# Attention of the first layer in pairs of heads, woven between its projections, with probabilities scaled by a diagonal on TensorE

## The chip, the cores and the metric

The kernel runs on one core of one Trainium2 chip. The metric is the time of one execution on the device in microseconds. An execution that was recorded by the hardware profiler shows where the time goes. The engines are TensorE (PE in the rows; its weight loads are PEld), VectorE (DVE), ScalarE (ACT), GpSimd (POOL) and SyncE (SP), whose queue issues nearly all loads.

## The reference

A trunk of two layers on 256 positions of width 1024, in fp32. Each layer is a mixer and a feed-forward block (SwiGLU, inner width 2816), both with norms in front and behind. The second layer's mixer (dilated attention) is not touched except in names. The first is a sparse attention with 16 query heads of 64, 4 key heads, and three branches for every head, each with a sigmoid gate:

```
proj = a @ w_in                                   # q 1024 | six k/v of 256 | gates 48
kc, vc = compress(k_cmp, wk1, wk2), compress(v_cmp, wv1, wv2)   # 15 blocks of 32 positions, stride 16
        # compress: silu(blocks(2048) @ w1(2048x256)) @ w2(256x64)
p_cmp = softmax(mask(q @ kc * scale)) * valid ;  o_cmp = p_cmp @ vc
o_sel = softmax(mask(q_rot @ k_sel * scale)) @ v_sel     # with 256 positions all blocks are selected
o_win = softmax(mask(q_rot @ k_win * scale)) @ v_win     # causal, window 512
o = g_cmp * o_cmp + g_sel * o_sel + g_win * o_win ;  m = o @ w_o
```

## The kernel before

Every engine has its own program, written out by hand; what stands earlier in an engine's program runs earlier, and semaphores order the engines against each other. There is no planner.

**Weights.** They come in pieces of 128x2048 fp32 into a ring of seven slots (`w_raw`). ScalarE writes the rounded high part (`split`, L606), VectorE the rest (`w_lo`, L1073). TensorE multiplies a block in three products, high by high, high by low, low by high (`three`, through `mm`, L1545). A slot is loaded again when `piece_used` says that its products are done. The pieces are in the order of `N_CMPKV ... N_NSAO, N_FFN0`.

**First layer.** The rows of x are transposed (L1554), with the gains `g_t` that come out of one transpose of `rows` (L1610). Then come ten projections of 128 positions by 512 columns (`nsa_gemm`), each 24 products: 0 to 5 for the keys and values, 6 to 9 for the queries. Between them stand the gate product, the turns of keys and queries, and `compress` for the keys and for the values (48 products of 256 columns each, both operands split into high and low).

**Attention.** It follows the last query projection. A unit is one head and one tile m of 128 queries; there are 32. For each unit TensorE makes the scores of both branches in one product (`scores_nsa`, L1738): the keys stand in `k_z` with zeros in the half of the 128 rows that belongs to the other head, so that the contraction is over 128 rows. VectorE adds the mask and takes the minimum of the negated scores (L1284), ScalarE exponentiates and sums (L804), VectorE takes the reciprocal (L1294) and multiplies the probabilities by it and by the gate (L1300). TensorE transposes them in blocks of 128 (`turn_probs`, L1761) into one of two banks, ScalarE copies the bank to `p_t` (L816), and TensorE multiplies by the values (`pv`, L1769), one head in columns 0 to 63 or 64 to 127 of the array, block after block. After each second head it adds the product with the compressed values (L1788). TensorE is three units behind its scores with the transposes and five with the values. GpSimd builds masks.

**Behind it.** `out_proj` (four blocks, 96 products) starts when all heads are done, then the norm and residual (`gain_post`, `add_post`), and the feed-forward block starts with the transposed rows `xt_hi`, `xt_lo` (L615, L1105).

The functions that the change touches, with the line numbers of the rows:

## Time and profile before

| | us |
|---|---|
| median of 3 runs | 864.36 (863.7 to 865.74) |
| the profiled execution | 866.18 |
| its span | 864.4 |
| TensorE busy in the span | 845.2 (98%) |
| VectorE / ScalarE / GpSimd busy | 535.4 / 476.1 / 37.5 |
| first layer's mixer, from the first product of a projection to the first feed-forward product | 11.17 to 191.80 |
| of it the attention | 94.4 to 166.9 |

The profiled execution's time is the one on the device; the span runs from its first recorded instruction to its last. A share of busy time over the whole span says little about a stage, so the rows below are by stretch and by piece. In a chain of waits every line is a piece of the path that ended last. A product of two fp32 operands shows as two records (x2 for one product), one of the rounded fp32r type as one, and a plain transpose as one. The duration of a record reaches past the start of the next; the lengths in the chain do not.

### The profile page before, as it was taken

To read this page: it belongs to the slowest core of one execution; us is meant where nothing else is said; L and a number is where in the kernel's file an instruction comes from. 1 tells how busy PE (TensorE), PEld (TensorE's weight loads), DVE (VectorE), ACT (ScalarE), POOL (GpSimd) and SP (SyncE) were. 2 spreads that over 40 slices of the span, in tenths; PEclk is the share of its full clock that TensorE was granted. 3 is DMA by queue.
4 is the path that set the end of the run, shared out by engine and by line. 5 is a ranking of instruction groups with operands and counts; after the bars stand their busy time and mean duration, and the time that the engine had idled before them with its cause. 6 is when DMAs were issued, how large, how long until landed. Compare 5 with 4: busy or idle time off the path is not lost.

```text
span 864.4 us, 11546 instructions
## 1 busy us (share of the span) xinstructions
PE 845.2 (98%) x4345; PEld 682.8 (79%) x4345; DVE 535.4 (62%) x1136; ACT 476.1 (55%) x862; POOL 37.5 (4%) x120
## 2 busy tenths in 40 slices
PE   6999999999999999999999999999999999999996
PEld 5898766778888888878887888888777888888885
DVE  5987786686655555578455555655566965455544
ACT  7786666664544444465555655665556754444431
POOL 3000018200000000000000000000000000000000
PEclk9999999999999999999999999999999999999999
DMA  9775300044565466468545353535331756645601
GB/s 323 243 258 193 98 1 2 1 156 159 183 228 175 148 219 217 146 197 272 190 155 185 98 183 110 167 126 174 119 98 50 238 187 222 205 147 191 223 24 49
DMA packets 108967, 137.48 MB, mean 159 GB/s; under 512 B 6336, under 2 KB 92400, under 8 KB 108784
## 3 DMA queue, kind: packets, MB, share of 16 engines
q1 hardware_dynamic: 107824, 132.53, 46.1%
q0 software_dynamic: 992, 4.19, 1.3%
q8 instruction: 34, 0.56, 0.3%
q14 instruction: 21, 0.17, 0.1%
q10 hardware_dynamic: 96, 0.02, 0.0%
HBM read 134.64 MB, written 2.10 MB: 158 GB/s over the span
## 4 chain that ended last, share of the span: by engine, by line
PE 92%; DVE 4%; ACT 2%; DMA 1%; issue 0%; ACTq 0%; SPq 0%
PE ps L1545 79%; PE ps L1554 5%; PE ps L1738 3%; PE ps L1769 3%; PE ps L1761 1%; DVE w_lo L1073 1%; DVE xt_lo L1105 1%; PE ps L1788 1%; DMA w_raw<-in_ffn_w_gu 1%; DMA rows<-in_nsa_cmp_pos 1%; ACT w_hi L606 0%; PE ps L1716 0%; ACT xt_hi L615 0%; DVE h L1347 0%; ACT probs L804 0%
## 5 line engine op out<-in xcount | busy, mean ns | idle before, releaser
L1073 DVE TENSOR_TENSOR w_lo<-w_raw,w_hi 128x1024 fp32r<-128x1024 f32 x248 | 296.5, 1222 | 116.1 <-ACT w_hi L606 114.1
L1545 PE MATMUL ps<-w_hi,xt_hi 128*128 128x512 f32 x760 | 309.0, 407 | 3.1 <-DVE xt_lo L1105 2.0
L1545 PE MATMUL ps<-w_hi,xt_lo 128*128 128x512 f32 x760 | 299.0, 393 | 0.0
L1545 PE MATMUL ps<-w_lo,xt_hi 128*128 128x512 f32 x760 | 298.3, 393 | 0.0
L606 ACT ACTIVATE w_hi<-w_raw 128x1024 fp32r<-128x1024 f32 x248 | 253.5, 1058 | 6.1 <-DMA w_raw<-in_ffn_w_gu 6.0
L1545 PEld LDWEIGHTS ps<-w_hi,xt_hi 128*128 128x128 f32 x760 | 144.3, 190 | 32.5 <-DVE xt_lo L1105 2.4
L1545 PEld LDWEIGHTS ps<-w_hi,xt_lo 128*128 128x128 f32 x760 | 144.2, 190 | 31.7
L1545 PEld LDWEIGHTS ps<-w_lo,xt_hi 128*128 128x128 f32 x760 | 144.6, 190 | 26.9
L871 ACT ACTIVATE st_hi<-ps 128x256 fp32r<-128x256 f32 x40 | 15.4, 384 | 116.8 <-PE ps L1554 116.8
L1377 DVE TENSOR_TENSOR st_lo<-ps,st_hi 128x256 fp32r<-128x256 f32 x40 | 17.0, 425 | 75.0 <-ACT st_hi L871 74.8
L1545 PE MATMUL ps<-w_hi,st_hi 128*128 128x512 f32 x160 | 62.6, 391 | 0.0
L1545 PE MATMUL ps<-w_hi,st_lo 128*128 128x512 f32 x160 | 62.3, 389 | 0.0
L1545 PE MATMUL ps<-w_lo,st_hi 128*128 128x512 f32 x160 | 62.3, 389 | 0.0
L804 ACT ACTIVATE probs<-probs,mn 128x128 f32<-128x128 f32 (+2 forms) x96 | 51.4, 537 | 15.5 <-DVE mn L1284 15.5
L866 ACT ACTIVATE silu<-ps,rs 128x256 f32<-128x256 f32 x44 | 20.9, 475 | 66.8 <-PE ps L1545 66.5
L959 ACT ACTIVATE qk_t<-ps 128x256 f32<-128x256 f32 x48 | 15.8, 382 | 53.5 <-PE ps L1554 53.5
L1371 DVE SCALAR_TENSOR_TENSOR hs<-ps,rs,silu 128x256 f32<-128x256 f32 x44 | 21.3, 483 | 34.1 <-ACT silu L866 34.1
L1545 PEld LDWEIGHTS ps<-w_hi,st_lo 128*128 128x128 f32 x160 | 30.0, 188 | 6.3
L1545 PEld LDWEIGHTS ps<-w_lo,st_hi 128*128 128x128 f32 x160 | 30.1, 188 | 6.1
L1545 PEld LDWEIGHTS ps<-w_hi,st_hi 128*128 128x128 f32 x160 | 30.0, 188 | 6.1
L1284 DVE CUSTOM_DVE_ANT_0 probs<-ps,mask_dil 128x512 f32<-128x512 f32 x32 | 20.8, 689 | 22.3 <-PE ps L1545 22.2
L1284 DVE CUSTOM_DVE_ANT_0 probs<-ps,mask_nsa 128x128 f32<-128x128 f32 (+1 forms) x64 | 20.2, 354 | 16.1 <-PE ps L1738 15.3
(206 smaller groups left out, 853.4 us busy)
## 6 DMA issues: line engine op xcount, KB each, us to landing
w_raw<-in_ffn_w_gu SPq DMA_DIRECT2D x88, 512.0 KB, 5.0
w_raw<-in_dil_w_in SPq DMA_DIRECT2D x72, 512.0 KB, 4.7
w_raw<-in_ffn_w_down SPq DMA_DIRECT2D x44, 512.0 KB, 4.7
w_raw<-in_nsa_w_in SPq DMA_DIRECT2D x20, 512.0 KB, 6.1
w_raw<-in_nsa_w_o SPq DMA_DIRECT2D x8, 512.0 KB, 4.7
w_raw<-in_dil_w_o SPq DMA_DIRECT2D x8, 512.0 KB, 4.5
w_raw<-in_nsa_cmp_wk SPq DMA_DIRECT2D x4, 512.0 KB, 9.7
w_raw<-in_nsa_cmp_wv SPq DMA_DIRECT2D x4, 512.0 KB, 6.7
```

The lines of the kernel that those rows point to most:

```text
L606: act.activation(w_hi[:, n.slot, c:c + 1024], w_raw[:, n.slot, c:c + 1024], ACT.Copy)\
L804: ins = act.activation(p, p, ACT.Exp, bias=mn[:, w % 4, br:br + 1], scale=-1.0, accum_out=l_u[:, w % 4, br:br + 1])
L866: act.activation(silu[:, m, :], bank(gu_bank(j, m), 0, 256), ACT.Silu, scale=rs[:, m:m + 1])\
L959: ins = act.activation(view(qk_t, (qk_slot(x.g, x.pat) * 4 + 2 * t) * S + x.m * 64, [[S, 2], [P, 2], [1, 64]]), view(ps, (2 + x.qk_no % 2) ...
L1073: dve.tensor_tensor(w_lo[:, n.slot, c:c + 1024], w_raw[:, n.slot, c:c + 1024], w_hi[:, n.slot, c:c + 1024].bitcast(F32), ALU.subtract)\
L1284: ins = dve.tensor_tensor_reduce(out=probs[:, w % 4, br * n:(br + 1) * n], in0=bank(score_bank(w) if b is None else b, br * n, n), in1=mas ...
L1371: dve.scalar_tensor_tensor(hs[:, m, :], bank(gu_bank(j, m), 256, 256), rs[:, m:m + 1], silu[:, m, :], ALU.mult, ALU.mult).then_inc(hs_read ...
L1377: dve.tensor_tensor(view(st_of(j)[1], m * P, [[S, 2], [1, P]]), bank(6 + m, 0, 256).rearrange("p (a t) -> p a t", a=2), hi.bitcast(F32), A ...
L1545: ins = pe.matmul(o, s, m, start=start, stop=stop)
L1554: ins = pe.transpose(ps[0:n, b, P * k:P * k + P], src, ident[:, :])
L1738: pe.matmul(bank(score_bank(u), 0, 2 * n), q_t[:, hd // 2, m * P:(m + 1) * P], k_z[:, hd % 2, :, hd // G, 0:n], start=True, stop=True).the ...
L1769: ins = pe.matmul(o, v, p_t[:, w % 4, P * k:P * k + P], start=k == 0, stop=i == 1 and k == len(vs) - 1, skip_group_check=i == 0)
```

## The change

Four things change, all in the first layer's mixer.

1. *Pairs.* The 32 units become 16 pairs of heads (`pair_nsa`: half r of the heads, tile m, pair j). Both heads of a pair stand in one tile of 128 rows of `q_t` and `k_both`, and their scores are products over 64 rows each, the one in rows 0 to 63, the other in 64 to 127, into two banks. The values are multiplied with the two heads alternating between the column halves. The products with the compressed values come four at a time, once for four pairs.
2. *Unscaled probabilities.* VectorE no longer multiplies the probabilities. It makes gate over sum, four numbers a pair and row; GpSimd multiplies the identity by them (`diag`, 128x512), and TensorE multiplies each block of probabilities by its diagonal in a full fp32 product, which transposes and scales it at once.
3. *Weaving.* The attention of pair s stands two pairs behind its scores, and between its parts stand quarters and eighths of the query projections 7 to 9 (`q_part`) and of the output projection (`o_part`), which used to stand before and behind.
4. *Compression and head.* The compression's weights are not split; keys and values are multiplied in plain fp32, in two column halves alternating. The gate product comes after the third projection; the rows of the gains are loaded and transposed in two parts; the second tile of x is transposed in the middle of the first projection.

Core of the diff (the score, mask and exponential steps of one pair, the diagonals, the products; of the written-out order two pairs):

```diff
+            for s in range(PAIRS_NSA):
+                pool.wait_ge(rl_ready, s + 1)
+                if s >= 2:
+                    pool.wait_ge(pt_psum[0], turns_nsa(s - 1))
+                pool.tensor_tensor(diag[:, s % 2, :, :], view(ident, 0, [[0, 4], [1, P]]),
+                                   view(rl, s % 4 * 4, [[1, 4], [0, P]]), ALU.mult).then_inc(normed[0], 1)
...
+            def attend(s, between=None):
+                if s >= 2:
+                    pt_out_nsa(turns_nsa(s - 2))
+                if s < PAIRS_NSA:
+                    exp_nsa(2 * s, P * (pair_nsa(s)[1] + 1))
+                if between:
+                    between()
+                if s >= 2 and pair_nsa(s - 2)[1]:
+                    pt_out_nsa(turns_nsa(s - 2) + 1)
+                if s < PAIRS_NSA:
+                    exp_nsa(2 * s + 1, P * (pair_nsa(s)[1] + 1))
...
-                    if gate is None:
-                        ins = dve.tensor_scalar(p, p, rl[:, w % 4, br:br + 1], None, ALU.mult)
-                    else:
-                        ins = dve.tensor_scalar(p, p, rl[:, w % 4, br:br + 1], gate, ALU.mult, ALU.mult)
...
+                link(dve.reciprocal(r_pair, l_u[:, at:at + 2, :]))
+                dve.tensor_tensor(r_pair, r_pair, view(gates, m * 48 + H + 8 * r + 2 * j, [[1, 2], [H, 2]]),
+                                  ALU.mult).then_inc(rl_ready, 1)
...
-                    ins = three(bank(b, 0, 256), tb_hi[:, kt, :, :].rearrange("p a b -> p (a b)"),
-                                tb_lo[:, kt, :, :].rearrange("p a b -> p (a b)"),
-                                w_hi[:, p.slot, c:c + 256], w_lo[:, p.slot, c:c + 256], kt == 0, kt == 15)
+                    for kv, w1 in enumerate((w1_k, w_raw)):
+                        if kt % 8 == 0:
+                            pe.wait_ge(raw_loaded[p.slot][kv], p.loaded())
+                        ins = mm(ps[64 * kv:64 * kv + 64, 3, 0:256],
+                                 tb[:, kt, kv, :, :].rearrange("p a b -> p (a b)"),
+                                 w1[:, p.slot, c:c + 256], kt == 0, kt == 15)
...
-                pe.matmul(bank(score_bank(u), 0, 2 * n), q_t[:, hd // 2, m * P:(m + 1) * P],
-                          k_z[:, hd % 2, :, hd // G, 0:n], start=True, stop=True).then_inc(scores[0], 1)
+                for odd in range(2):
+                    hd, rows = 8 * r + 2 * j + odd, slice(DH * odd, DH * odd + DH)
+                    pe.matmul(bank(score_bank(odd), 0, 2 * n), q_t[rows, hd // 2, m * P:(m + 1) * P],
+                              k_both[rows, :, hd // G, 0:n], start=True, stop=True).then_inc(scores[0], 1)
...
+            def probs_nsa(s, odd):
+                m, k = pair_nsa(s)[1], turns_nsa(s) + odd
+                pe.wait_ge(normed[0], s + 1)
+                if k:
+                    pe.wait_ge(pt_out[0], k)
+                for i in range(4):
+                    w, c = (2 * s + odd, P * i) if m else (2 * s + i // 2, P * (i % 2))
+                    t, at = probs_of_nsa(w)
+                    ins = mm(bank(PT_BANK, P * i, P), t[:, at, c:c + P],
+                             diag[:, s % 2, 2 * odd + i // 2 if m else i, :], True, True)
+                ins.then_inc(pt_psum[0], 1)
...
+                for i in range(2 * (m + 1)):
+                    for odd in range(2):
+                        at, c = ((k + odd) % 2, P * i) if m else (k % 2, P * (2 * odd + i))
+                        pe.matmul(view(ps, OT_BANK * 512 + P * j, [[1, P]], p0=DH * odd, n=DH),
+                                  v_nsa[:, i // (m + 1), i % (m + 1), hk * DH:(hk + 1) * DH],
+                                  p_t2[:, at, c:c + P], start=i == 0 and j == 0, stop=False, skip_group_check=True)
...
+            scores_nsa(10)
+            o_nsa(0, 1, 2)
+            probs_nsa(8, 0)
+            o_nsa(0, 1, 3)
+            values_nsa(8)
```

Three places in the order show what moved. The first is TensorE in the middle of the attention. Before, `k_z` is the scores, `ident,probs` the transposes, `p_t,v_nsa` the values and `pc_t,vc_bd` the compressed values:

```order
L1738 MATMUL ps<-k_z,q_t 128x256 [waits masked0]
L1761 MATMUL ps<-ident,probs 128x128 [waits pt_out0,normed0]
L1761 MATMUL ps<-ident,probs 128x128 x3
L1769 MATMUL ps<-p_t,v_nsa 64x128 [waits pt_out0]
L1769 MATMUL ps<-p_t,v_nsa 64x128
L1738 MATMUL ps<-k_z,q_t 128x512 [waits masked0]
```

And now, where `k_both` is the scores of a pair, `w_hi,xt_hi` an eighth of the output projection, and `diag,probs_b` the product with the diagonals:

```order
L1815 MATMUL ps<-k_both,q_t 128x256 [waits masked0]
L1815 MATMUL ps<-k_both,q_t 128x256
L1599 MATMUL ps<-w_hi,xt_hi 128x512 [waits proj_out0,ot_ready0,lo_ready]
L1599 MATMUL ps<-w_lo,xt_hi 128x512
L1599 MATMUL ps<-w_hi,xt_lo 128x512
L1599 MATMUL ps<-diag,probs_b 128x128 [waits pt_out0,normed0]
L1599 MATMUL ps<-diag,probs_b 128x128 x3
```

A unit's own three steps followed each other; now projection products stand between the steps of different pairs, and the wait for `normed0` is one for GpSimd instead of VectorE.

The second place is VectorE at the same stage, before: mask (`mn`), reciprocal and the two multiplications of a unit.

```order
L1284 ISA probs,mn<-ps,mask_nsa 128x256 [waits pt_psum0,scores0]
L1284 ISA mn 128x1
L1284 ISA probs,mn<-ps,mask_nsa 128x256
L1284 ISA mn 128x1
L1294 RECIPROCAL rl<-l_u 128x2 [waits expd0]
L1300 TENSOR_SCALAR probs<-probs,rl,gates 128x128 [waits dve_step]
L1300 TENSOR_SCALAR probs<-probs,rl,gates 128x128
```

Now, between the fifth and the sixth pair, with half a weight split and a query rotation in the queue:

```order
L1286 ISA probs,mn<-ps,mask_nsa 128x256 [waits pt_psum0,scores0]
L1286 ISA mn 128x1
L1286 ISA probs,mn<-ps,mask_nsa 128x256
L1286 ISA mn 128x1
L1107 TENSOR_TENSOR w_lo<-w_raw,w_hi 128x1024 [waits hi_ready]
L1188 TENSOR_TENSOR rope_a<-stage_rot,cos_107 128x128 [waits proj_out0]
L1189 TENSOR_TENSOR rope_b<-stage_rot,sin_108 128x8x8
L1191 TENSOR_TENSOR rope_b<-stage_rot,sin_108 128x8x8
L1193 TENSOR_TENSOR stage_rot<-rope_a,rope_b 128x8x16 [waits dve_step]
L1309 RECIPROCAL rl<-l_u 128x4 [waits normed0,expd0,roped0]
L1310 TENSOR_TENSOR rl<-rl,gates 128x4 [waits dve_step]
```

The two multiplications of 128 or 256 columns are gone, one of four columns is new, and splits and rotations stand between a mask and the next reciprocal.

The third place is TensorE from the last key projection (`xt_hi`) into the compression, before:

```order
L1545 MATMUL ps<-w_lo,xt_hi 128x512
L1545 MATMUL ps<-w_hi,xt_lo 128x512
L1545 MATMUL ps<-w_hi,tb_hi 128x256 [waits lo_ready,tb_ready,gate_exp]
L1545 MATMUL ps<-w_lo,tb_hi 128x256
L1545 MATMUL ps<-w_hi,tb_lo 128x256
```

Now, with a turn of keys (`ident,stage_nsa`) in front, `w_k` the weights of the keys and `w_raw` those of the values:

```order
L1599 MATMUL ps<-w_hi,xt_lo 128x512
L1608 MATMUL ps<-ident,stage_nsa 128x128 [waits roped0,pair_dve]
L1608 MATMUL ps<-ident,stage_nsa 128x128 x3
L1599 MATMUL ps<-w_k,tb 64x256 [waits raw_loaded1_0,gate_exp,tb_ready]
L1599 MATMUL ps<-w_raw,tb 64x256 [waits raw_loaded1_1]
L1599 MATMUL ps<-w_k,tb 64x256
```

Three products of 128 rows out became one of 64, alternating between keys and values, and the wait for the split parts became one for the load.

## Rows read from the trace of the kernel before

**Rows 1.** Stretches: busy us of PE, PEld, DVE, ACT, POOL; granted clock; DMA share, GB/s.

```profile
64.20:191.80 127.60, 124.03 (x684) 92.80 (x682) 93.46 (x315) 82.90 (x226) 27.75 (x88) 1.00 0.23 76
190.00:200.00 10.00, 8.20 (x29) 6.59 (x30) 7.52 (x33) 5.57 (x13) 0.55 (x1) 0.83 0.67 215
```

**Rows 2.** Chain of waits inside the attention: start us, us, what.

```profile
106.77 1.02 PE ps L1769 x8
107.79 0.63 PE ps L1738 x2
...
109.65 0.41 PE ps L1788 x2
...
110.70 0.44 PE ps L1761 x4
111.13 0.58 PE ps L1769 x4
111.71 1.05 PE ps L1738 x2
```

**Rows 3.** What TensorE waited for: us in total, times, longest.

```profile
PE ps L1545 <- DVE xt_lo L1105: 2.0, 1, 2.0
...
PE ps L1761 <- ACT q_t L682: 1.0, 1, 1.0
PE ps L1738 <- ACT stage_rot L668: 0.6, 1, 0.6
```

**Rows 4.** TensorE in order of time, second layer: start us, us, tiles.

```profile
481.58 1.15 PE L1545 MATMUL ps<-qk_t 64*128 64x256 f32 x12
...
486.63 1.09 PE L1545 MATMUL ps<-p_t,v 128*64 128x128 f32 x16
```

**Rows 5.** Chain of waits, compression and start of the attention.

```profile
58.61 5.75 PE ps L1545 x48
...
87.59 1.71 PE ps L1716 x16
89.30 0.94 PE ps L1738 x4
```

**Rows 6.** VectorE by line, 64.2 to 191.8 us: xcount | busy us, mean ns | idle before.

```profile
L1073 DVE TENSOR_TENSOR w_lo<-w_raw,w_hi 128x1024 fp32r<-128x1024 f32 x22 | 26.0, 1220 | 5.3 <-ACT w_hi L606 5.0
L1300 DVE TENSOR_SCALAR probs<-probs,rl,gates 128x256 f32<-128x256 f32 x32 | 12.9, 445 | 0.6
...
L1300 DVE TENSOR_SCALAR probs<-probs,rl,gates 128x128 f32<-128x128 f32 x32 | 10.2, 361 | 0.6
...
L1311 DVE TENSOR_TENSOR xt_lo<-ps,xt_hi 128x512 fp32r<-128x512 f32 x4 | 2.7, 680 | 3.0 <-ACT xt_hi L810 3.0
```

**Rows 7.** ScalarE by line, the same stretch.

```profile
L804 ACT ACTIVATE probs<-probs,mn 128x256 f32<-128x256 f32 x32 | 15.9, 500 | 1.3 <-DVE mn L1284 1.3
...
L816 ACT ACTIVATE p_t<-ps 128x512 f32<-128x512 f32 x16 | 9.5, 597 | 13.3 <-PE ps L1761 13.3
...
L810 ACT ACTIVATE xt_hi<-ps 128x512 fp32r<-128x512 f32 x4 | 2.3, 587 | 2.3 <-PE ps L1788 2.3
```

**Rows 8.** GpSimd by line, the whole span.

```profile
L544 POOL MEMSET k_z<- 64x2048 f32 x2 | 3.6, 1800 | 0.1
...
L566 POOL TENSOR_SCALAR_AFFINE_SELECT mask_dil<-mask_dil 128x256 bf16<-128x256 bf16 x2 | 0.8, 409 | 0.3 <-POOL mask_dil L562 0.2
```

**Rows 9.** Chain of waits, the head of the program.

```profile
1.73 5.20 DMA rows<-in_nsa_cmp_pos
```

**Rows 10.** The three small loads of the gains.

```profile
DMA to landing us min/median/max: 2.9/3.8/5.2
```

**Rows 11.** VectorE by line, 102 to 122 us, then 128 to 156 us.

```profile
L1300 DVE TENSOR_SCALAR probs<-probs,rl,gates 128x256 f32<-128x256 f32 x8 | 2.9, 410 | 0.1
...
L1300 DVE TENSOR_SCALAR probs<-probs,rl,gates 128x256 f32<-128x256 f32 x13 | 5.2, 438 | 0.2
```

**Rows 12.** A stretch of the second layer, columns as in Rows 1.

```profile
600.00:610.00 10.00, 10.00 (x68) 7.86 (x67) 6.18 (x13) 5.81 (x12) 0.00 (x0) 1.00 0.52 182
```

More of the change, by code:

```diff
@@ L542, in _ @@
             link(pool.memset(kc_bd[:, :, :], 0.0))
-            for par in range(2):
-                link(pool.memset(k_z[64 - 64 * par:128 - 64 * par, par, :, :, :], 0.0))
             link(pool.memset(bd_mask[:, :], 1.0))
@@ L793, in _ @@
+            cmp_exp(1)
+            attend(12)
             split(15, (1,))
[L794 to L806 removed]
@@ L838, in _ @@
-            ot_evac(HK - 1)
+            attend(13, between=lambda: cmp_turned(1))
+            split(16, (0,))
+            ot_hi_nsa(2)
+            attend(14)
+            split(16, (1,))
+            attend(15)
+            split(17, (0,))
             def post_squares(b, m, halves=(0, 1)):
@@ L1235, in _ @@
[L1235 to L1244 removed]
+            split(7)
@@ L1272, in cmp_probs @@
                    .then_inc(pc_ready, 1)
-            rope(0, 9, stage_rot, 0, 8, 0)
-            split(15)
-            cmp_scores(0)
-            cmp_less_max(0)
-            def mask_unit(i, w, n, masks, b=None):
-                dve.wait_ge(scores[i], w + 1)
-                if w >= 4:
-                    dve.wait_ge(pt_psum[i], w - 3)
-                for br, mask in enumerate(masks):
-                    ins = dve.tensor_tensor_reduce(
-                        out=probs[:, w % 4, br * n:(br + 1) * n], in0=bank(score_bank(w) if b is None else b, br * n, n),
-                        in1=mask, scale=1.0, scalar=INF, op0=ALU.add, op1=ALU.min,
-                        accum_out=mn[:, w % 4, br:br + 1])
-                ins.then_inc(masked[i], 1)
@@ L1331, in _, with mask_part, mask_pair_nsa @@
-            split(16)
-            ot_lo(HK - 1)
+            def mask_part(dst, w, c, n, mask, least):
+                return dve.tensor_tensor_reduce(out=dst, in0=bank(score_bank(w), c, n), in1=mask, scale=1.0,
+                                                scalar=INF, op0=ALU.add, op1=ALU.min, accum_out=least)
+            def mask_pair_nsa(s):
+                n = P * (pair_nsa(s)[1] + 1)
+                for w in (2 * s, 2 * s + 1):
+                    dve.wait_ge(scores[0], w + 1)
+                    if s >= 4:
+                        dve.wait_ge(pt_psum[0], turns_nsa(s - 3))
+                    t, at = probs_of_nsa(w)
+                    for br in range(2):
+                        ins = mask_part(t[:, at, br * n:(br + 1) * n], w, br * n, n, mask_nsa[:, 2 * P - n:2 * P],
+                                        mn[:, w % 8, br:br + 1])
+                    ins.then_inc(masked[0], 1)
@@ new lines, in _ @@
+            hid_silu()
+            split(10)
+            rope(0, 7, stage_rot, 0, 8, 0)
+            hid_copies()
+            split(11, (0,))
+            dve.wait_ge(masks_ready, 4)
+            mask_pair_nsa(0)
+            vc_blocks()
+            mask_pair_nsa(1)
+            rope(0, 8, stage_rot, 1, 8, 1)
+            norm_nsa(0)
+            mask_pair_nsa(2)
+            split(11, (1,))
+            norm_nsa(1)
+            mask_pair_nsa(3)
+            split(12)
+            cmp_scores(0)
@@ new lines, in _ @@
+            norm_nsa(7)
+            mask_pair_nsa(9)
+            split(14, (1,))
+            norm_nsa(8)
+            ot_lo_nsa(1)
+            mask_pair_nsa(10)
+            norm_nsa(9)
+            mask_pair_nsa(11)
+            split(15, (0,))
+            cmp_scores(1)
+            norm_nsa(10)
+            mask_pair_nsa(12)
+            cmp_probs(1)
+            norm_nsa(11)
+            mask_pair_nsa(13)
+            split(15, (1,))
+            norm_nsa(12)
+            ot_lo_nsa(2)
+            mask_pair_nsa(14)
@@ L1603, in _, with turn_x @@
             pe.wait_ge(ident_ready, 1)
-            for m in range(MT):
+            pe.wait_ge(rows_loaded[0], 16)
+            pe.transpose(bank(2, 0, 16), rows[0][:, :], ident[0:16, 0:16]).then_inc(rows_t, 1)
+            def turn_x(m):
                 pe.wait_ge(x_loaded[m], 16)
```

873 lines of the change are left out of this document (480 added, 393 removed).

## The prediction

> **What bounds the kernel now.** I read four views in this order. First the busy time by stretch [rows 1]: between the end of the compression and the start of the first feed-forward block, 64.2 to 191.8 us, TensorE is busy 124.0 of 127.6 us, VectorE 93.5, ScalarE 82.9, GpSimd 27.8. So the stretch is as long as TensorE's own work, and it shrinks only if that work shrinks or if new waits are kept below what is saved. Second the chain of waits inside the attention [rows 2]: it runs from one TensorE piece to the next, with no other engine between. The reader sees there what each piece of a head and query tile costs: scores 0.63 us (256 keys) and 1.05 (512 keys), which is 0.21 fixed plus 0.42 for each 256 columns; four plain transposes 0.44; value products 0.58 for two and 1.02 for four; the product with the compressed values 0.41. Third, who waited for whom [rows 3]: in this stretch TensorE waits for others 0.6, 1.0 and 2.0 us, no more. Fourth the same kinds of products in the second layer [rows 4], where two heads alternate: sixteen value records (eight products of 128 columns, the two heads in different column halves) take 1.09 us, while layer one needs 1.02 for four such products of one head. Twelve score records of 64 rows (512 keys for each of two heads) take 1.15, and layer one needs 1.05 for 512 keys of one head. Two heads in different halves of the array therefore run side by side, at the price of one.
>
> **TensorE's work, part by part.** The 32 units (one head, one query tile) become 16 pairs, eight with one key block (m=0) and eight with two (m=1).
> Scores: before 16 x 0.63 + 16 x 1.05 = 26.9. Now the two heads of a pair use row halves of 64, alternating, as in [rows 4]: 8 x 0.63 + 8 x 1.05 = 13.4. Gain 13.5.
> Values: before 16 x 0.58 + 16 x 1.02 = 25.6. Now a pair of m=1 is word for word the 1.09 group of [rows 4], a pair of m=0 half of it with its fixed part, 0.6: 8 x 1.09 + 8 x 0.6 = 13.5. Gain 12.1.
> Compressed values: before 16 lone products of 0.41 = 6.6; now four groups of four, each 4 x 0.21 + 0.2 = 1.05, so 4.2. Gain 2.4.
> Compression: before two runs of 48 products, 5.75 each [rows 5], 11.5. Now 32 fp32 products of 256 columns, key and value side in different column halves: 32 x 0.42 / 2 + 0.2 = 6.9. Gain 4.6; 32 x 0.42 = 13.4 if the halves did not overlap, a loss of 1.9.
> Probabilities: before 96 transposes, 16 x 0.22 + 16 x 0.44 = 10.6. Now 96 full fp32 products of a 128x128 block with a diagonal, in 24 groups of four (eight records). No row shows a run of such. From below: a transpose group, 0.44. From above: a lone product with a 128-column weight and 128 columns streamed, 0.41 [rows 2], four times, 1.64. Between them lie the runs of [rows 5]: sixteen records with full weights and 32 columns take 1.71, 0.107 each, and four with 256 columns 0.94, 0.235 each, which is nearly what streaming alone costs (0.21). In both, loading a weight is hidden behind the record before it or the other way round, so eight records of 128 columns cost 8 x 0.107 + 0.1 = 0.95. I take 0.95, nearest to the run of sixteen: 24 x 0.95 = 22.8, a loss of 12.2 (bounds 0 and 28.8).
> Sum of TensorE's work: -13.5 - 12.1 - 2.4 - 4.6 + 12.2 = -20.4 (the projections, the gate product, the remaining turns and the output projection are the same products in another order). The eight splits of the compression weights fall away on ScalarE and VectorE, but before 64.2 us, under TensorE's projections: no gain.
>
> **The other engines.** VectorE loses the two multiplications of every unit, 12.9 + 10.2 us [rows 6], and gets 16 small products of sum and gate; in the stretch it then has some 70 us of work. ScalarE keeps its exponentials, 0.50 and less each, and copies 24 full banks of 0.60 instead of 16 full and 16 half ones [rows 7]: about 82 us as before. TensorE has 124.0 - 15.8 (the sum without the compression) = 108. So on the average TensorE stays the bound, with ScalarE at 75%.
> GpSimd gets 16 builds of 128x512 fp32 from two inputs. Its trace has no such row. An affine_select of 256 columns takes 0.41 [rows 8], doubled for 512 columns 0.82, doubled again for a second input 1.64; a memset of 2048 columns takes 1.8. Bounds 0.41 and 1.8, value 1.2, midway between the two doublings. 16 x 1.2 = 19 us in 100 is no load; it counts only as a delay in each pair's chain. What stood in its queue moves behind the last build: the load of the post-norm gain, still needed only after the output projection, and the masks of the second layer, hundreds of microseconds early in either order. The loads' queue gains two pieces of room in its ring of seven; with the DMA 0.23 busy in the stretch [rows 1] that costs nothing. The Trainium skill, "GPSIMD Engine Reference", section 3.1, gives 4497 ns for a two-input fp32 product of 2048 elements, which would make 1.12 us here (an estimate) and the same sum.
> Per pair the chain is scores, mask, exponentials, reciprocal and gate, build, product, copy, values. TensorE takes up the product of pair s only after the scores of s+2. Its 108 us less some 34 at both ends are 4.6 us a pair; two turns less the scores themselves are 8.2. The chain's own parts are at most mask 1.4, exponentials 2.0 (four of 0.50, [rows 7]), reciprocal and gate 0.4, build 1.2: 5.0. A half split queued ahead, 1.22 on VectorE [rows 6] and about 1.1 on ScalarE, makes 7.3. Cover of some 1 us is left where one falls on both engines.
>
> **Waits that go, waits that come.** Going: 0.6 and 1.0 of [rows 3], since the last query projection no longer stands alone in front of the attention. -1.6. Coming, walked through by order and durations: the first product with a diagonal, because pair 0 has only a score and a few projection products in front of it, 1.3; the compressed scores behind a full split and a query evacuation on ScalarE, 1.2; two products with compressed values that wait for a copy queued behind an exponential, 0.4 and 0.8; and the last four steps of the output projection, which wait for the last pair's result to be copied and split, 0.59 + 0.68 [rows 6, 7], 1.3. Together 5.0. The entry to the feed-forward block waits 2.0 now [rows 3] and keeps it: the splits stand ahead of the transposed rows on VectorE in either order, 0.2 more. The fall of the granted clock there (0.83 between 190 and 200 us, [rows 1], 1.7 us lost, right behind the wait of 2.0) also stays.
>
> **The head.** Before, the chain starts with the third of three small loads, 5.2 us under way [rows 9]; the gains of all norms wait for it, and ScalarE's first transposed rows wait for them. The landing times of the three loads are 2.9, 3.8 and 5.2 [rows 10]. Now the first transpose needs only the first load, issued first, and the next bound is x itself. First load instead of third is 2.3 us earlier, so the first product can move at most that far ahead; the weights' arrival and VectorE's queue (the gate split, the angles) take part of it back. I take 1.5; bounds 0 and 2.3.
>
> **A rule against the change.** While GpSimd ran affine_selects nearly without a break, 128 to 156 us, VectorE's in-place multiplications of 256 columns went from 410 to 438 ns [rows 11]; that is all the contention this trace shows. The Trainium skill, "SBUF — State Buffer", section "SBUF: two separate sides", says that a VectorE operation with two SBUF inputs and a GpSimd operation that reads SBUF exclude each other for their whole length. The trace bears it out only as a few per cent. As a mechanism of this kernel: a build that meets a split (two SBUF inputs, 1.22) starts up to 1.22 later, and a split that meets a build up to 1.2 later. For the likeliest case I add 1.7, about one such hold at each of the places with the least cover that shows up on TensorE for half its length; holding at every pair is a rival below.
>
> **The sum.** The profiled execution took 866.18 us, 1.8 more than its span of 864.4 and 1.8 more than the median of the runs, 864.36. 866.2 - 20.4 (work) - 1.6 (waits gone) - 1.5 (head) + 5.2 (waits come) + 1.7 (holds) = 849.6, and on the scale of the median 847.8. I predict 848 us.
>
> **Rivals.**
> 1. *The queues of ScalarE and VectorE lengthen each pair.* Splits and evacuations stand at fixed places between the exponentials; where one of each falls into the same pair, the cover of 1 us is used up. For: ScalarE at 75% with long pieces. Against: the second layer is woven like this, and TensorE is busy there through ten microseconds of ten [rows 12]. Nine of the fourteen woven pairs with 1 us each: +9, 857. Chance 0.17.
> 2. *Weights are not hidden in the products with a diagonal.* Then a group costs 4 x 0.41 = 1.64: 24 x 0.69 = +16.6, 864.5, no change. For: every lone fp32 product shows a fixed part of 0.21. Against: both runs of [rows 5]. Chance 0.07.
> 3. *The build closes the loop (slower than before).* Place: the wait of TensorE for the diagonal of pair s; the build waits in turn for the products of pair s-2 to release its buffer. Price: a build of 1.8 held by one split of 1.22 is 3.0, 1.8 above my value and 0.9 above the cover, at 16 pairs +14; waits of that length can lower the clock as the 2.0 of [rows 1, 3] did, 1.7 for perhaps five of them, +8.5: 871. It decides from an average wait of 1 us a pair on; above that nothing of the 16.5 us is left. Chance 0.06.
> 4. *More is hidden than I walked.* The coming waits vanish but for the entry, the head gives 2.3: 842. Chance 0.10.
>
> **How the numbers follow.** Forecast 0.60, with its own range 843 to 854. Cases 4, 1 and part of 2 fill 840 to 861; what is left out is most of 2, 3 and some surprise, less than 0.2. A measurement of this kernel tells no change from one of about 0.2%, 1.7 us. Faster than 862.6: forecast, 1, 4 and a part of 2, 0.89. Within: half of 2 and a rest, 0.05. Slower: 3, 0.06.
>
> **What would show it.** In the profile after: groups of score, value and diagonal records of 1.05, 1.09 and 0.95 us; a compression of about 7; TensorE waiting for the build only at the first pair; the first feed-forward product at some 174 to 176 us instead of 191.8, and nothing changed behind it but by that shift. Wrong would be: value or score records that follow each other singly; diagonal groups near 1.6; waits of TensorE for GpSimd in most pairs; a granted clock below full in the woven stretch.

## The result, and the profile after

The changed kernel took 858.0 us (median of 4, 857.4 to 858.5), the kernel before on the same chip 865.0: ratio 0.992, interval 0.9903 to 0.9937. Measured again, on the chip of repaired_early below, it was 0.9933 (0.992 to 0.9947). The forecast of 848 (840 to 861) had the direction, and the range holds the time, but the gain is 7 us and not 16.5, and the forecast's own range without its rivals (843 to 854) does not hold it. The profiled execution took 857.36 instead of 866.18 us: 8.8 less, and this is what is taken apart below. By the medians it is 7.0 here and 5.6 in the second measurement: the kernel before took 863.2 to 865.7 in its other executions (one slow one left out), so the profiled one is its longest.

Stretches of the changed kernel, columns as in [rows 1]: from the end of the compression to the first feed-forward product, and the entry of that block.

```profile
60.30:181.87 121.57, 114.19 (x780) 85.09 (x778) 67.28 (x244) 80.49 (x219) 32.70 (x52) 1.00 0.24 79
180.00:190.00 10.00, 8.13 (x29) 6.60 (x30) 9.52 (x34) 4.62 (x9) 8.63 (x21) 0.83 0.72 227
```

The first row is 121.6 us where [rows 1] has 127.6; TensorE is busy 114.2, and 108 was forecast. The first feed-forward product starts at 181.87 instead of 191.80. The clock falls to 0.83 at the entry, as in [rows 1].

What TensorE waited for in the changed kernel, the answer to [rows 3].

```profile
PE ps L1599 <- DVE w_lo L1107: 4.0, 3, 2.8
...
PE ps L1599 <- DVE xt_lo L1139: 2.0, 1, 2.0
PE ps L1599 <- DVE xt_lo L1323: 1.4, 1, 1.4
PE ps L1599 <- ACT qu_t L703: 1.3, 1, 1.3
PE ps L1853 <- ACT pc_t L773: 1.1, 2, 0.9
PE ps L1608 <- DVE stage_dil L1497: 1.0, 1, 1.0
PE ps L1599 <- POOL diag L573: 0.9, 1, 0.9
```

The build is waited for once (0.9, the first pair), as forecast; 1.3, 1.1, 1.4 and 2.0 are the other four waits that were walked. More than before are the 4.0 at the head and the 1.0 in the second layer.

Groups of VectorE and GpSimd in the first stretch, columns as in [rows 6]: the splits and the builds.

```profile
L1107 DVE TENSOR_TENSOR w_lo<-w_raw,w_hi 128x1024 fp32r<-128x1024 f32 x20 | 24.3, 1233 | 6.9 <-ACT w_hi L625 6.7
...
L573 POOL TENSOR_TENSOR diag<-ident,rl 128x512 f32<-128x512 f32 x16 | 16.7, 1041 | 141.9 <-DVE rl L1310 141.9
```

A build takes 1.04 (1.2 forecast), and a split in this stretch 1.23 ([rows 6] 1.22).

TensorE's time, kind by kind. A block is a run of records of one kind with nothing between; it is counted from the start of its first record to the start of the next block, less a wait shown there.

| us | before | after | difference | forecast |
|---|---|---|---|---|
| start to the end of the compression | 64.20 | 60.41 | -3.8 | -6.1 |
| 192 projection records behind it | 44.6 | 52.4 | **+7.8** | 0 |
| scores | 23.5 | 13.5 | -10.0 | -13.5 |
| values | 25.1 | 13.0 | -12.0 | -12.1 |
| compressed values | 6.64 | 3.76 | -2.9 | -2.4 |
| probabilities | 13.5 | 21.0 | +7.5 | +12.2 |
| turns and the rest | 10.7 | 11.0 | +0.3 | 0 |
| waits shown | 3.6 | 6.7 | +3.1 | +3.6 |
| holds by the build | | | 0 | +1.7 |
| first feed-forward product to the end | 672.62 | 673.76 | +1.1 | 0 |
| sum | | | -8.9 | -16.6 |

(The sum is 0.1 off the measured 8.8 by rounding.) Attention's own products gained 17.4 where 15.8 was forecast. The loss is in the line that was costed at nothing. How it looks, in order of time on TensorE in the changed kernel (start, duration, tiles):

```profile
109.16 0.50 PE L1599 MATMUL ps<-w_hi,xt_hi 128*128 128x512 f32 x1
109.49 0.40 PE L1599 MATMUL ps<-w_lo,xt_hi 128*128 128x512 f32 x1
109.73 0.40 PE L1599 MATMUL ps<-w_hi,xt_lo 128*128 128x512 f32 x1
109.96 1.05 PE L1599 MATMUL ps<-diag,probs 128*128 128x128 f32 x8
110.77 0.47 PE L1599 MATMUL ps<-w_hi,xt_hi 128*128 128x512 f32 x1
111.09 0.39 PE L1599 MATMUL ps<-w_lo,xt_hi 128*128 128x512 f32 x1
111.31 0.40 PE L1599 MATMUL ps<-w_hi,xt_lo 128*128 128x512 f32 x1
111.80 1.13 PE L1599 MATMUL ps<-diag,probs 128*128 128x128 f32 x8
```

Read the starts, not the durations. Inside a run projection records follow each other every 0.23. Here three of them take 0.80 from 109.16 to 109.96, and 1.03 from 110.77 to 111.80, instead of 0.68. What a block takes beyond 0.228 for each of its records is called its excess below. No wait is shown beside the second group, since the modelled duration of the record ahead of it (0.40, to 111.71) hides most of it. ScalarE's copy of the bank between the two diagonal groups:

```profile
111.05 0.60 ACT L812 ACTIVATE p_t<-ps 128x512 f32<-128x512 f32 x1 [2.72 <-PE ps L1599]
```

It ends at 111.65, and the second group, which needs the bank, starts 0.15 later. So in 1.03 there are 0.68 of work and two other things: a price of changing to another kind of product, and a hidden wait for the copy. The experiments separate them.

### The profile page after: what moved, and what is told of

It reads as the page before. It is cut to its first block, busy times and chain, and to the rows that moved or that the text cites. A ratio compares the mean times of both kernels' runs of the same rounds, so it can differ in the third digit from the quotient of the medians.

```text
span 855.6 us, 11604 instructions
## 1 busy us (share of the span) xinstructions
PE 830.9 (97%) x4410; PEld 667.5 (78%) x4410; DVE 503.2 (59%) x1062; ACT 460.5 (54%) x840; POOL 62.0 (7%) x134
## 4 chain that ended last, share of the span: by engine, by line
PE 90%; DVE 5%; ACT 3%; issue 1%; DMA 0%; POOL 0%; ACTq 0%; POOLq 0%; DVEq 0%
PE ps L1599 82%; PE ps L1608 5%; PE ps L1841 1%; DVE w_lo L1107 1%; PE ps L1815 1%; ACT w_hi L625 1%; DVE xt_lo L1139 1%; ACT probs L797 1%; PE ps L1853 0%; DMA h<-in_x 0%; ACT xt_hi L634 0%; DVE h L1399 0%; DVE h L1403 0%; DVE tmp L1401 0%; ACT probs_b L797 0%
## 5 line engine op out<-in xcount | busy, mean ns | idle before, releaser
L1107 DVE TENSOR_TENSOR w_lo<-w_raw,w_hi 128x1024 fp32r<-128x1024 f32 x240 | 288.2, 1225 | 116.3 <-ACT w_hi L625 114.2
L1599 PE MATMUL ps<-w_hi,xt_hi 128*128 128x512 f32 x760 | 312.8, 412 | 7.5 <-DVE w_lo L1107 4.0
L625 ACT ACTIVATE w_hi<-w_raw 128x1024 fp32r<-128x1024 f32 x240 | 245.8, 1057 | 0.6 <-DMA w_raw<-in_nsa_w_in 0.5
L1599 PEld LDWEIGHTS ps<-w_hi,xt_hi 128*128 128x128 f32 x760 | 144.5, 190 | 44.1 <-issue 11.7
L993 ACT ACTIVATE qk_t<-ps 128x256 f32<-128x256 f32 x48 | 15.8, 382 | 55.9 <-PE ps L1608 55.9
L593 POOL TENSOR_SCALAR_AFFINE_SELECT mask_dil<-mask_dil 128x128 bf16<-128x128 bf16 x80 | 34.4, 430 | 5.5
L807 ACT ACTIVATE probs<-probs,mn 128x512 f32<-128x512 f32 x32 | 23.0, 718 | 13.4 <-DVE mn L1286 13.4
```

The lines of the kernel that those rows point to most:

```text
L593: link(pool.affine_select(out=pd, in_=pd, compare_op=ALU.not_equal, fill=0.0, base=-d, pattern=[[-1, P]], channel_multiplier=1))
L625: act.activation(w_hi[:, n.slot, c:c + 1024], w_raw[:, n.slot, c:c + 1024], ACT.Copy)\
L807: act.activation(p, p, ACT.Exp, bias=mn[:, w % 4, 0:1], scale=-1.0, accum_out=l_u[:, w % 4, 0:1]).then_inc(expd[1], 1)
L993: ins = act.activation(view(qk_t, (qk_slot(x.g, x.pat) * 4 + 2 * t) * S + x.m * 64, [[S, 2], [P, 2], [1, 64]]), view(ps, (2 + x.qk_no % 2) ...
L1107: dve.tensor_tensor(w_lo[:, n.slot, c:c + 1024], w_raw[:, n.slot, c:c + 1024], w_hi[:, n.slot, c:c + 1024].bitcast(F32), ALU.subtract)\
L1599: ins = pe.matmul(o, s, m, start=start, stop=stop)
```

## The experiments

All ratios are to the kernel before on the same chip; the changed kernel has 0.992 to 0.9933.

**Is it the switch or the copy? (short_copy)**

```diff
-                act.activation(p_t2[:, k % 2, :], bank(PT_BANK), ACT.Copy)
+                n = 512 if k < 2 else 64
+                act.activation(p_t2[:, k % 2, 0:n], bank(PT_BANK, 0, n), ACT.Copy)
```

> The changed kernel, but after the first two groups ScalarE copies only 64 of the 512 columns of each bank of scaled probabilities (it leaves out most of that copy; the value products read what stood there). In the changed kernel the 192 projection records between the compression and the feed-forward block take 54.5 us, 10.7 more than 192 x 0.228. Theory A (switching): most of the 10.7 is a price of each change between projection records and another kind of product, 0.10 to 0.20 us a block whatever anybody waits for; then only the excess above that goes away (6 blocks between two diagonal groups at 0.35, 14 blocks before values at 0.25 to 0.35): projections 52 us, the time 2 to 3 us less, about 855.5. Theory B (hidden wait): the excess is nearly all a wait for ScalarE's copy of the single bank, which the list of TensorE's waits hides because a record's duration reaches past the next start; then the projections fall to 45 or 46 us and the time by 8 to 9, about 849.5.

Measured 0.9888 (0.987 to 0.9906). TensorE at the same place of this kernel:

```profile
109.52 1.05 PE L1600 MATMUL ps<-diag,probs 128*128 128x128 f32 x8
110.33 0.47 PE L1600 MATMUL ps<-w_hi,xt_hi 128*128 128x512 f32 x1
110.65 0.39 PE L1600 MATMUL ps<-w_lo,xt_hi 128*128 128x512 f32 x1
110.87 0.40 PE L1600 MATMUL ps<-w_hi,xt_lo 128*128 128x512 f32 x1
111.10 1.05 PE L1600 MATMUL ps<-diag,probs 128*128 128x128 f32 x8
```

Three records between two diagonal groups now take 0.77, an excess of 0.09 (0.35 before the edit). Nobody waits there: the short copy ends at 110.83, and the group starts 0.27 later, not 0.15.

```profile
110.61 0.22 ACT L813 ACTIVATE p_t<-ps 128x64 f32<-128x64 f32 x1 [3.06 <-PE ps L1600]
```

In front of values the excess is 0.19 in all eleven blocks (0.25 to 0.35 before), and in front of a diagonal behind scores 0.12 as before. The projections take 50.1 us. (The 54.5 and 10.7 of the expectation held the wait of 2.0 at the entry too; without it they are 52.4 and 8.7.) So 2.3 us were hidden waits for the copy, and 6.4 of excess stay although nobody waits: theory A. The kernel before had 0.9 of it in 7 blocks; now there are 42 blocks. Switching costs 5.5 us. The time by itself, 853.4, lies between the two theories (855.5 and 849.5); the excess decides. In the profiled executions it fell by 3.9: beside the 2.3, the groups with a diagonal took 0.6 less and the waits for a copy of the compressed probabilities 0.5 less.

Passing a semaphore or starting a new bank is not the price: in the kernel before, the run of 84 such records from 166.87 to 186.05, with both inside it, has an excess of 0.04 in all.

The kernel before shows the price where projections alternate with two transposes in the feed-forward block; nothing is waited for there.

```profile
213.55 0.39 PE L1545 MATMUL ps<-w_hi,st_lo 128*128 128x512 f32 x1
213.78 0.38 PE L1554 MATMUL ps<-ident,hs 128*128 128x128 f32 x2
213.92 0.48 PE L1545 MATMUL ps<-w_hi,xt_hi 128*128 128x512 f32 x1
214.23 0.39 PE L1545 MATMUL ps<-w_lo,xt_hi 128*128 128x512 f32 x1
214.46 0.40 PE L1545 MATMUL ps<-w_hi,xt_lo 128*128 128x512 f32 x1
```

The record behind the transposes needs 0.31 until the next one starts, the others 0.23. By the blocks of the changed kernel: 0.09 to 0.13 to come back from another kind, 0.1 more to leave for scores or values, which use a part of the array, nothing more to leave for a diagonal. The Trainium skill, "TensorE: Matmul & The Clock Gate", section "Step-by-step: what each phase is for", lets one product's drain overlap the next one's fill, so that only the columns count in a stream; the trace agrees inside a run of one kind (0.23 for 512 columns) and not at a change of kind. Whether the number type, the part of the array or the weights make the price was not separated.

**Fewer, larger pieces (merged)**

```diff
             scores_nsa(8)
-            o_nsa(0, 0, 1)
             probs_nsa(6, 0)
-            o_nsa(0, 0, 2)
+            o_nsa(0, 0, 1, 2)
             probs_nsa(6, 1)
```

> The changed kernel, but in eight of the sixteen pairs the two pieces of projection in front of and behind the first diagonal group stand together behind it: eight blocks of projection records fewer, the same products. Theory A (switching): 8 x 0.12 = 1.0 us less from the blocks themselves, and where the joined block stands between two diagonal groups (5 pairs) or before values (3 pairs) the copy is covered too, 5 x 0.23 + 3 x 0.06 = 1.3: together -2.3, projections 52.2 us, about 855.7. Theory B (hidden wait): only the eight covered copies count, 8 x 0.25 to 0.35 = -2.4 with the block number worth nothing; the blocks in front of a diagonal group keep an excess of 0.12 in A and would have none in B. Rival to both: the first diagonal group, now directly behind the scores, comes before its build is ready, and the wait moves there: no change or up to +3.

Measured 0.9906 (0.989 to 0.9921), median 855.2. The five joined blocks between two diagonal groups have an excess of 0.09 to 0.11, and TensorE still waits for the build only once. Size and place are as theory A has them; the time agrees (855.7 forecast), but its interval overlaps that of the changed kernel.

**No weaving of the output projection (unwoven)**

```diff
             probs_nsa(5, 1)
-            o_nsa(0, 0, 0)
             values_nsa(5)
...
             compressed_nsa(3)
+            o_nsa(0, 0, 0, 1, 2, 3)
...
```

All 23 such lines of pairs 5 to 15 go behind the last compressed values.

> The changed kernel, but the 23 pieces of the output projection that stand between the parts of pairs 5 to 15 stand behind the last pair, as one run (ScalarE and VectorE take the squares and the gain behind it too). Theory A (switching): projections fall from 54.5 to about 47 us. But the copies of the probabilities lie bare: some 14 to 18 times 0.9 us, +13 to +16. Sum: +5 to +9, about 865. Theory B (hidden wait): the same bare copies, and the projection time falls to 46 as well; the two differ little here. Rival: weaving is worth nothing, since what it hides it gives back in switches: 856 to 860.

Measured 1.0087 (1.0071 to 1.0103): 13 us slower than the changed kernel, where 5 to 9 were expected. Its projections take 47.0, as forecast, and the copies lie bare:

```profile
155.06 1.13 PE L1598 MATMUL ps<-diag,probs 128*128 128x128 f32 x8 [0.78 <-ACT p_t L812]
156.88 1.09 PE L1840 MATMUL ps<-p_t,v_nsa 128*64 128x128 f32 x16 [0.69 <-ACT p_t L812]
157.91 1.16 PE L1598 MATMUL ps<-diag,probs_b 128*128 128x128 f32 x8
159.84 1.13 PE L1598 MATMUL ps<-diag,probs_b 128*128 128x128 f32 x8 [0.78 <-ACT p_t L812]
```

Waits of 0.69 to 0.84 in the pairs 5 to 15, 11.7 us in 16 places by the list of waits; by the starts each is about 1.0 (from 155.06 to 156.88 are 1.82, and a group takes 0.81). So weaving the output projection saves 13 us, its price already paid.

**The orders that were wrong (three_fixes)**

VectorE at the head and at the entry, TensorE in the second layer (ScalarE's splits of pieces 18 and 19 move with VectorE's):

```diff
             split(2)
+            split(3)
...
-            split(3)
             split(4)
...
             gain_post(1, 0)
+            split(18, (0,))
             ot_lo_nsa(3)
             add_post(1, 0)
-            split(18)
-            split(19, (0,))
             xt_lo_out(1, 0, 0, 2)
-            split(19, (1,))
             xt_lo_out(1, 0, 1, 2)
+            split(18, (1,))
+            split(19, (0,))
             gain_post(1, 1)
             add_post(1, 1)
             h_rs(1, 0)
+            split(19, (1,))
...
-                    if e > 4:
-                        dil_turn(TILES[e - 1])
+                    dil_turn(TILES[e - 1])
```

> The changed kernel with the order repaired at three places that the prediction had wrong, each to be read by itself. Head: VectorE splits piece 3 before the gate's weights and the angles, so that the wait of 1.15 us in the middle of the third projection goes: -1.0. Entry to the feed-forward block: half of the split of piece 18 stands in front of the last attention result (both engines idle there for 2 to 4 us), the rest of the splits of pieces 18 and 19 behind the transposed rows, and one piece of the output projection stands behind the last compressed values: first feed-forward product 3.5 us earlier in relation to the last group, of which 1 is given back when TensorE comes to pieces 18 and 19: -2.5. Second layer: the turn of its fourth tile back into the middle of the fifth projection: the wait of 1.0 us goes, -1.0. Sum -4.5, about 853.5. Rival: each wait only moves to the next one in the queue (the gate's product, the second half of the feed-forward rows, the next tile): -1 or less, 857.

Measured 0.9867 (0.9844 to 0.9889), median 851.2. The wait in the third projection is gone (from the end of the first projection to the end of the third 11.8 us instead of 12.8), the wait of 1.0 in the second layer is gone, and at the entry only 0.5 is waited for the last copy and 0.5 for piece 19; the granted clock stays at 1.00 there. The time fell by as much as expected or more, so the rival, that each wait only moves on, is out. How the second layer lost its 1.1 in the changed kernel (ScalarE, VectorE, TensorE in order of time):

```profile
402.27 0.60 PE L1608 MATMUL ps<-ident,stage_dil 128*128 128x128 f32 x4
...
402.91 0.66 ACT L993 ACTIVATE qk_t<-ps 128x256 f32<-128x256 f32 x2 [4.29 <-PE ps L1608]
...
404.40 0.69 ACT L972 ACTIVATE stage_dil<-ps,rs 128x512 f32<-128x512 f32 x1
...
406.28 0.29 DVE L1497 TENSOR_TENSOR stage_dil<-rope_a,rope_b 128x128 f32<-128x128 f32 x1
...
406.63 0.55 PE L1608 MATMUL ps<-ident,stage_dil 128*128 128x128 f32 x3 [0.99 <-DVE stage_dil L1497]
```

The turn of the fourth tile, moved behind a whole projection, comes at 402.27; ScalarE's copy of it stands in its queue in front of the evacuation of the next tile, which starts at 404.40, and that tile's turn is then 0.99 late.

**The price of the diagonal (plain_turns)**

```diff
-                    ins = mm(bank(PT_BANK, P * i, P), t[:, at, c:c + P], diag[...], True, True)
+                    ins = turn(PT_BANK, i, t[:, at, c:c + P])
```

> The changed kernel, with the 96 products by a diagonal replaced by plain transposes of the unscaled probabilities (GpSimd builds the diagonals all the same and TensorE waits for them as before; what is left out is the multiplication by gate over sum). It prices the term 'probabilities', forecast 24 x 0.95 in place of 10.6. If a diagonal group costs TensorE its 0.87 us and a transposing group 0.40, the time falls by 24 x 0.47 = 11, to 0.979 of the kernel before (0.992 now). Rival: TensorE is not the bound in these pairs; the queues of ScalarE and VectorE (their chain was ready 1.06 us early at pair 2 and 0.05 early at pair 11) take most of it back: 0.987 or more.

Measured 0.9839 (0.9824 to 0.9853): 7 to 8 us, not 11. TensorE's 24 groups fell from 21.0 to 9.5 us; the waits within the pairs grew by 1.3, and the granted clock of the profiled execution was 0.85 and 0.81 in 80 to 100 us, where TensorE is busy only 7.5 of the first 10 us. So the term is near its forecast (21.0 for 22.8), and part of the gain is lost to the other engines and the clock; how much to each is not shown.

**The cover of a pair (double_build)**

```diff
+                link(build())
                 build().then_inc(normed[0], 1)
```

> The changed kernel, with GpSimd building each diagonal twice (1.04 us more, and a semaphore between, in every pair). It tests the cover of about 1 us that the prediction gave each pair, and its rival 3. If the cover is there in most pairs: TensorE waits for the build at three to six of the sixteen places, 0.3 to 1.2 us each, +3 to +5 us, 0.996 to 0.998. If the loop is closed already: 16 x 1.1 = +17, 1.012. If the cover is far larger than 1 us: +1.1 at the first pair alone, 0.993. VectorE's splits of 1.22 us are to be read beside it: if a build and a split held each other for their length, splits that meet a build would take up to 2.3 us; the changed kernel shows 1.22 to 1.23.

Measured 0.9965 (0.995 to 0.9979). TensorE waits for the build at two pairs:

```profile
PE ps L1601 <- POOL diag L573: 3.8, 2, 3.0
```

That is 2.9 more than in the changed kernel, 2.1 of it at the first pair; 14 of 16 pairs hide a build of 2.1. Fewer places than expected: the cover is above 1.1 nearly everywhere, and rival 3 is far off. The first pair lost more than the 1.1 of a second build, because there the second build met a split on VectorE (GpSimd, then VectorE):

```profile
78.27 3.13 POOL L573 TENSOR_TENSOR diag<-ident,rl 128x512 f32<-128x512 f32 x2 [73.62 <-DVE rl L1312]
...
79.28 1.23 DVE L1109 TENSOR_TENSOR w_lo<-w_raw,w_hi 128x1024 fp32r<-128x1024 f32 x1 [0.33 <-ACT w_hi L627]
...
80.63 0.80 DVE L1312 TENSOR_TENSOR rl<-rl,gates 128x4 f32<-128x4 f32 x1
```

The first build takes 1.04; the second starts at 79.39, after the split, and takes 2.02. The split takes its usual 1.23. Then VectorE's product of four columns, 0.17 elsewhere, starts at 80.63 while the build runs and takes 0.80, to the end of the build. So whichever came second was held. It is the only build of the 32 that stood beside a split for more than 0.03 us.

**The head (turn_early)**

```diff
             turn_x(0)
+            turn_x(1)
...
             def turn_rest():
-                turn_x(1)
```

> The changed kernel, with the second tile of x transposed in front of the first projection again instead of in its middle. The changed kernel starts its first product 1.84 us earlier (9.33 instead of 11.17), yet the first projection ends at 18.55 in both. Theory: records run at half pace (0.43 instead of 0.228) until about 14.6 us in both kernels, so the earlier start only adds slow records, and the transposes stand in the open in the middle for 1.1 us. Then the early turn gives back some of it: first product at 10.6, fourteen fast records and no turn behind 14.6: first projection ends at 17.8 to 18.0, -0.6, ratio 0.991. Rival: half pace lasts a certain time from the first product on, or the weights' splits come too late: the end stays at 18.5 or moves to 19, ratio 0.992 to 0.993.

Measured 0.991 (0.9891 to 0.9929), not to be told from the changed kernel. In the trace the first projection ends at 18.09 instead of 18.55, the wait in the third is gone as well (11.8 us from there to the end of the third projection), and the compression ends 1.5 earlier; the first feed-forward product starts 1.65 later all the same, behind 80 to 100 us at a granted clock of 0.80 and 0.86 and 170 to 180 at 0.83 in this profile.

**All together (repaired, repaired_early; the changed kernel again)**

```diff
-            split(12)
             turn_q(0, 1, 1, 2)
+            split(12)
...
-            attend(13, between=lambda: cmp_turned(1))
+            cmp_turned(1)
+            attend(13)
```

These two on ScalarE stand beside the edits of three_fixes and merged; repaired_early has the early turn as well.

> The three repairs and the eight joined blocks together, and two more in ScalarE's queue: the query evacuation in front of the split of piece 12 (TensorE waited 1.3 us for it), and the copies of the compressed probabilities in front of the exponentials (waits of 0.2 and 0.9). If the effects add: -5.2 (three repairs) -1.3 (joined) -1.3 -1.1 = -8.9 from the changed kernel, ratio 0.982, and no fall of the granted clock at the entry of the feed-forward block. Rival: the waits move on to the next instruction in the same queue (the build of pair 2, the exponentials of pair 13): ratio 0.985 or more.

> All repairs and the second tile of x turned in front of the first projection. If the head's two effects are separate, the early turn adds 0.5 us to the repairs (the first projection ended at 18.09 instead of 18.55 with it): ratio 0.9797 where the repairs alone had 0.9802, hardly to be told apart. If it only brought the same wait of 1.15 us to an end that the split order already ends: 0.980 to 0.981.

> The changed kernel once more, on the chip of the run above, so that the repairs are compared with it directly: 0.992 of the kernel before, its interval 0.9903 to 0.9937; the granted clock between 80 and 100 us, 1.00 in its profile and 0.80 to 0.88 there in four of the variants, may be either.

Measured: repaired 0.9802 (0.9787 to 0.9816), median 847.4; repaired_early 0.9805 (0.9792 to 0.9819), 846.9, on the chip where the changed kernel had 857.8 and 0.9933. So with the early turn it is 10.9 us faster than the changed kernel on one chip (8.9 expected of the repairs alone); the early turn adds nothing that can be told. What TensorE still waits for in the repaired kernel:

```profile
PE ps L1601 <- DVE w_lo L1108: 3.8, 3, 2.8
...
PE ps L1601 <- POOL diag L573: 2.1, 2, 1.2
PE ps L1601 <- DVE xt_lo L1324: 0.5, 1, 0.5
```

The waits of 1.3, 1.1 and 2.0 and the 1.0 in the second layer are gone, there are two for the build (2.1) where there was one of 0.9, and the clock at the entry is 1.00.

## Why the prediction was right and wrong

**What bounds: right.** TensorE stayed the bound (busy 114.2 of 121.6 us); the double build shows the cover. Rival 1 named 857, about the time that came, but not for its reason: the listed waits in the pairs are the forecast ones, and of hidden waits for ScalarE there are 2.3 us, where the rival had 9.

**Sizes of the products: right.** A diagonal group takes 0.80 to 0.92, the first 0.99 (forecast 0.95), so rival 2 is out; scores 0.63 and 1.06, values 0.59 and 1.03; the compression 53.35 to 60.41, 7.1 (6.9). What was off are the pieces of the kernel before. The prediction took their lengths from the chain, scores 26.9 and transposes 10.6; by the starts they are 23.5 and 13.5, since the two views divide the border between two kinds differently. Scores gained 3.5 less and probabilities lost 4.7 less than forecast: that these two nearly cancel is no merit of the sum.

**The step that failed** is the bracket behind the sum of TensorE's work: "the projections, the gate product, the remaining turns and the output projection are the same products in another order", costed at nothing. Cut into 42 blocks they took 7.8 us more: 5.5 for switching (shown by short_copy) and 2.3 of waits for the copy of the one bank that three records don't cover. The prediction's look at a woven stretch, [rows 12], "busy there through ten microseconds of ten", could not have seen it: with records of 0.39 that start every 0.23, TensorE is busy all the time with or without the price.

**Waits that come: right.** 4.7 by the trace (0.9, 1.3, 1.1, 1.4 and the same 2.0 at the entry), 5.2 forecast.

**Holds by the build: not there.** 1.7 was added; the builds take 1.040 to 1.043. But 15 of the 16 met no split at all, and the first met one for 0.03 us: on VectorE the split of a pair stands ahead of the reciprocal that releases its build. During 13 of the builds VectorE does nothing, during the others it makes masks. So it was the order that kept the two apart, which the prediction did not work out. Where a build did meet a split, in double_build, it was held (2.02 instead of 1.04). The rule of the Trainium skill, "SBUF — State Buffer", section "SBUF: two separate sides", has the later of two such operations blocked until the earlier one ends; the trace agrees there, and this change gave it nothing to hold. The "few per cent" that the prediction read from [rows 11] are of multiplications of one tensor by a number a row, not of operations with two tensors from SBUF, and say nothing for or against it. The figure that the prediction takes from the Trainium skill, "GPSIMD Engine Reference", section 3.1, stands there for an add, not a product; the estimate from it, 1.12, is near the 1.04.

**The head: wrong.** Forecast -1.5, measured +0.7 (-3.8 with the compression's -4.5). The first product does start 1.84 earlier, but records go at half pace there (0.43 instead of 0.23) until 15.1 us before and 14.6 after, so twelve slow records stand where there were nine, the turn of the second tile now stands in the open for 1.1, and the gate product, moved away, no longer covers VectorE's queue in front of the split of piece 3 (some 1.0). About one microsecond of it can be chance: in the second profile of the changed kernel half pace ends after seven records, at 12.5 us, and the compression ends at 59.45, which makes the head -0.2. By these profiles the forecast is missed by 1.3 to 2.2.

**Behind the entry: wrong.** "Nothing changed behind it" overlooked one moved line of the diff, the turn of the fourth tile: +1.1, shown by its return in three_fixes.

In sum: 7.8 + 2.2 + 1.1 + 0.3 (projections, head, behind the entry, turns) worse than forecast, 1.7 + 1.6 + 0.5 (holds, products, waits) better: 7.6 of the 7.8 between 16.6 and 8.8. That the repaired kernel takes 847 shows that the waits were not inherent; it is no merit of the forecast.

## What to carry to other kernels

Work that is cut into pieces to be woven is not free: count the changes of kind, price each from a place in the same trace where two kinds alternate (0.09 to 0.2 us here), and make pieces as long as the copy that they must cover (0.6 us and its way there and back, some 1.0). Read a busy TensorE by the distance of its starts, since a share of 100% hides both. And follow every moved line of a diff into the queue in which it now stands, in the layer that seems untouched as well.

## What the hardware showed beside it

The start of full pace at the head differs from execution to execution. In the repaired kernel, whose records there are those of the changed kernel:

```profile
11.12 0.63 PE L1601 MATMUL ps<-w_lo,xt_hi 128*128 128x512 f32 x1
11.54 0.63 PE L1601 MATMUL ps<-w_hi,xt_lo 128*128 128x512 f32 x1
11.97 0.53 PE L1601 MATMUL ps<-w_hi,xt_hi 128*128 128x512 f32 x1
12.34 0.40 PE L1601 MATMUL ps<-w_lo,xt_hi 128*128 128x512 f32 x1
12.57 0.39 PE L1601 MATMUL ps<-w_hi,xt_lo 128*128 128x512 f32 x1
```

Starts are 0.43 apart until 12.0 us and 0.23 from 12.3 on; in the changed kernel 0.43 lasts to 14.6 in one profile and to 12.5 in the other, and the granted clock of the rows is 1.00 throughout, so the rows don't show the reason. That alone moves the end of the first projection of the changed kernel by 0.95 us (17.60 and 18.55).

The granted clock behind the waits at 79 to 86 us is not settled by the kernel either. The changed kernel, second profile:

```profile
80.00:90.00 10.00, 8.71 (x63) 6.68 (x64) 5.39 (x18) 7.42 (x23) 1.86 (x2) 0.88 0.61 214
90.00:100.00 10.00, 10.00 (x56) 6.50 (x56) 6.91 (x30) 6.08 (x18) 1.26 (x2) 0.95 0.01 2
```

In its first profile both stretches have 1.00, with TensorE busy 8.6 and 9.9. And GpSimd's affine_selects of 128 columns, at 168 to 207 us in the changed kernel, took 294 to 1377 ns, 430 in the mean, where the kernel before had 300 in a stretch without splits. Every one above 1.1 us stood beside a split (two tensors from SBUF) and ended 0.15 behind it; six of those splits took 1.30 to 1.31 instead of 1.22.
